# A two-layer diffusion step on one core: the first modulation vectors by matrix products, and a shorter last normalisation

## What is computed

```
m = silu(c) @ w_ada + b_ada                 # shift, scale, gate for each sublayer
u = x * (1 + scale) + shift
x = LN(ALPHA * x + res_w * gate * f(u))     # f: SwiGLU or mixing
```

## Time and profile before

| | |
|---|---|
| median of three runs | 2925.35 us (2923.78 to 2927.16) |
| the profiled execution: its own time | 2927.19 us |
| its span, first to last instruction | 2925.2 us |
| TensorE busy | 2786.0 us, 95% |
| VectorE busy | 1707.3 us, 58% |
| ScalarE busy | 774.8 us, 26% |
| mean granted TensorE clock | 0.983 of full speed |
| TensorE leaves the opening | at 117.93 us |
| the last reciprocal ends, the first block is multiplied | at 2904.08 us |

### The profile page before, as it was taken

How to read it: one execution, slowest core, us unless ns; L and a number is a source line. 1 busy time by engine, 2 the same in 40 slices (tenths; PEclk the granted TensorE clock), 3 DMA queues, 4 the chain that set the end, 5 groups by cost and what they waited for, 6 DMA issues and landing times.

```text
span 2925.2 us, 47407 instructions
## 1 busy us (share of the span) xinstructions
PE 2786.0 (95%) x18760; PEld 2740.6 (94%) x18760; DVE 1707.3 (58%) x3134; ACT 774.8 (26%) x1109; POOL 0.2 (0%) x4
## 2 busy tenths in 40 slices
PE   4899999899999999999999999989999999999994
PEld 4899999889999999999999999988989999999993
DVE  6654555753766773545586455575366568444456
ACT  3212111532322431111252111234232234111124
POOL 0000000000000000000000000000000000000000
PEclk8999999899999999999999999999999999999997
DMA  6343333112233232323223333321213322233220
GB/s 246 119 129 114 118 122 108 65 62 75 87 118 127 72 119 83 115 86 116 88 90 125 108 122 119 111 94 48 74 51 137 129 87 99 89 105 111 101 86 36
DMA packets 77061, 299.34 MB, mean 102 GB/s; under 512 B 24960, under 2 KB 29312, under 8 KB 52864
## 3 DMA queue, kind: packets, MB, share of 16 engines
q1 hardware_dynamic: 50688, 214.31, 21.0%
q10 hardware_dynamic: 26240, 83.20, 8.5%
HBM read 293.80 MB, written 6.82 MB: 103 GB/s over the span
## 4 chain that ended last, share of the span: by engine, by line
PE 89%; DVE 6%; issue 2%; ACT 1%; DMA 1%; SPq 0%; ACTq 0%; DVEq 0%
PE psum L588 12%; PE psum L590 12%; PE psum L591 12%; PE psum L406 6%; PE psum L409 6%; PE psum L408 6%; PE psum L451 3%; PE psum L454 3%; PE psum L455 3%; PE psum L808 3%; PE psum L810 3%; PE psum L811 3%; PE psum L492 2%; PE psum L497 2%; PE psum L496 2%
## 5 line engine op out<-in xcount | busy, mean ns | idle before, releaser
L588 PE MATMUL psum<-Uh,w_hi 128*128 128x320 f32 x2304 | 713.4, 310 | 8.9 <-DVE cst_l L1470 8.9
L590 PE MATMUL psum<-Ul,w_hi 128*128 128x320 f32 x2304 | 713.2, 310 | 0.0
L591 PE MATMUL psum<-Uh,w_lo 128*128 128x320 f32 x2304 | 713.0, 309 | 0.0
L872 ACT ACTIVATE w_hi<-w_raw 128x2048 fp32r<-128x2048 f32 x170 | 325.1, 1913 | 595.4 <-PE psum L406 318.8
L588 PEld LDWEIGHTS psum<-Uh,w_hi 128*128 128x128 f32 x2304 | 433.6, 188 | 9.2 <-issue 9.2
L1199 DVE TENSOR_TENSOR w_lo<-w_raw,w_hi 128x2048 fp32r<-128x2048 f32 x170 | 389.4, 2291 | 78.6 <-ACT w_hi L872 74.1
L590 PEld LDWEIGHTS psum<-Ul,w_hi 128*128 128x128 f32 x2304 | 433.7, 188 | 0.0
L591 PEld LDWEIGHTS psum<-Uh,w_lo 128*128 128x128 f32 x2304 | 433.6, 188 | 0.0
L1382 DVE TENSOR_TENSOR hf<-sg,psum 128x320 f32<-128x320 f32 x176 | 85.6, 486 | 407.6 <-ACT sg L960 406.1
L409 PE MATMUL psum<-Hh,w_lo 128*128 128x320 f32 x1024 | 316.2, 309 | 0.0
L406 PE MATMUL psum<-Hh,w_hi 128*128 128x320 f32 x1024 | 316.2, 309 | 0.0
(11 more groups left out here) (239 smaller groups left out, 5080.4 us busy)
## 6 DMA issues: line engine op xcount, KB each, us to landing
w_raw<-in_wstream SPq DMA_DIRECT2D x188, 1024.0 KB, 4.9
ada_w<-in_ada ACTq DMA_DIRECT2D x145, 512.0 KB, 3.6
first_w<-in_ada SPq DMA_DIRECT2D x15, 512.0 KB, 14.6
gath<-in_rpb SPq DMA_DIRECT2D x128, 24.0 KB, 3.3
G<-gath ACTq DMA_DIRECT2D x4, 768.0 KB, 4.5
X<-in_xT SPq DMA_DIRECT2D x8, 320.0 KB, 14.5
yT<-X SPq DMA_DIRECT2D x8, 320.0 KB, 3.4
mask<-in_mask ACTq DMA_DIRECT2D x2, 384.0 KB, 5.0
```

Source lines behind the costliest of these rows:

```text
L588: m1 = pe.matmul(out, wh, rh, start=(k == 0), stop=False)
L590: pe.matmul(out, wh, rl, start=False, stop=False)
L591: mm = pe.matmul(out, wl, rh, start=False, stop=(k == KD - 1))
L872: act.activation(hi, w_raw[:, r, :, :], ACT.Copy).then_inc(s_whi, 1)
```

## The change

Four things are changed.

1. The shift and scale of the first sublayer come from TensorE. c and c_ctx are loaded as columns (`ccol`, 128 x 8 x 2, 8 KB) and their silu `scol` is the moving operand of two columns; the slices of w_ada come in another layout (`ada_first`) and are the stationary operand. `mods_of(k)` makes 16 products in full f32 for block k into PSUM bank 6 or 7, and VectorE adds the bias in two small instructions (`first_mod`). All 16 slices now have buffers of their own, so no load waits. The two broadcasts are still needed by the sums of later sublayers; they are issued after block 4.
2. Both token halves of a block are made and used before the next block: three uses (tile 0 with both halves, tile 1 with the first) run block by block; tile 1 with the second half and the tiles 2 and 3 with both come after. The two weight tiles are loaded ahead of block 1.
3. TensorE's wait for the constants moves from the end of the opening to the first mixing.
4. In the last sublayer no u is made, by ScalarE or VectorE, in either half, and each half of each block is stored when it is ready, in 16 DMAs of 160 KB.

```diff
@@ SyncE
-            for k in range(2):
-                first_block(k)
+            first_block(0)
             for s in range(2):
                 sp.dma_start(w_raw[:, s, :, :], a["wstream"][s]).then_inc(s_wload[s], 16)
-            for k in range(2, 6):
+            for k in range(1, KD):
                 first_block(k)
-            sp.wait_ge(s_first, first_mods_ready(1, 1))
-            first_block(6)
-            first_block(7)
...
-            sp.wait_ge(s_y, DEPTH * PER_LAYER["y"])
-            for k in range(KD):
-                sp.dma_start(a["yT"][k], X[:, k, :]).then_inc(s_out, 16)
+            for h in range(2):
+                for k in range(KD):
+                    cols = slice(h * HT, (h + 1) * HT)
+                    sp.wait_ge(s_y, DEPTH * PER_LAYER["y"] - 2 * KD + (h * KD + k + 1))
+                    sp.dma_start(a["yT"][k][:, cols], X[:, k, cols]).then_inc(s_out, 16)
@@ TensorE, opening
+                def mods_of(k):
+                    pe.wait_ge(s_ada0[k], 32)
+                    if k == 0:
+                        pe.wait_ge(s_scol, 1)
+                    if k >= 2:
+                        pe.wait_ge(s_first, k - 1)
+                    for j in range(2):
+                        for c in range(KD):
+                            mm = pe.matmul(first_mods(k)[:, 2 * j:2 * j + 2], first_w[2 * k + j][:, c, :], scol[:, c, :],
+                                           start=(c == 0), stop=(c == KD - 1))
+                    mm.then_inc(s_fsum, 1)
...
+                mods_of(0)
+                mods_of(1)
                 tiles = [take(), take()]
...
                 for k in range(KD):
...
+                    if 1 <= k < KD - 1:
+                        mods_of(k + 1)
+                    pe.wait_ge(s_u, C["u"].at() + (2 * k + 1))
+                    block_products(tiles[0], us[0], 0, k)
+                    block_products(tiles[1], us[1], 0, k)
+                    pe.wait_ge(s_u, C["u"].at() + (2 * k + 2))
+                    block_products(tiles[0], us[2], 1, k)
+                one(tiles[1], 1)
+                late = take(spare_f)
+                one(late, 0, 2)
+                one(late, 1)
                 late = take(spare_h)
-                one(late, 0, 2)
-                one(late, 1, 1)
+                one(late, 0, 1)
+                one(late, 1)
                 C["u"].next(2 * KD)
-                pe.wait_ge(s_init, 4)
-                pe.wait_ge(s_cst, 64)
@@ ScalarE, finish
+                    if (l, s) != (DEPTH - 1, 2):
...
@@ VectorE, normalise
-                    split_u(h, k)
+                    if last:
+                        C["u"].next()
+                        C["u32"].next()
+                    else:
+                        split_u(h, k)
@@ VectorE, opening
+                def first_mod(k):
+                    dve.wait_ge(s_fsum, k + 1)
                     for j in range(2):
-                        if taken[0]:
-                            dve.wait_ge(s_first, taken[0])
-                        start_at = (bada[:, k:k + 1], lnm[:, 0, 0, k:k + 1])[j]
-                        dve.tensor_tensor_reduce(junk[:, :], first_w[(2 * k + j) % 12], csilu[:, v, :], 1.0, start_at,
-                                                 ALU.mult, ALU.add, mods[0][:, v, j * KD + k:j * KD + k + 1])\
-                            .then_inc(s_first, 1)
-                        taken[0] += 1
+                        i = dve.tensor_scalar(mods[0][:, :, j * KD + k], first_mods(k)[:, 2 * j:2 * j + 2],
+                                              (bada[:, k:k + 1], lnm[:, 0, 0, k:k + 1])[j], None, ALU.add)
+                    i.then_inc(s_first, 1)
```

More of the change, by code:

```diff
@@ L150, in build @@
         spare_o = [spare("spare_o0", 0, 8192), spare("spare_o1", 16384, 24576)]
-        craw = at("craw", 5120, [P, 2, D])
         cst = at("cst", 33792, [P, 4, P])
         warm = at("warm", 49152, [P, 1])
-        first_w = [at(f"first_w{i}", off, [P, D])[:, :] for i, off in enumerate(
-            (21504, 25600, 29696, 40960, 45056, 58880, 62976, 67072, 79360, 83456, 87552))]
-        first_w.append(ada_w[:, 1, :])
+        ccol = at("ccol", 49184, [P, KD, 2])
+        scol = at("scol", 49248, [P, KD, 2])
+        first_w = [at(f"first_w{i}", off, [P, KD, P])[:, :, :] for i, off in enumerate(
+            (21504, 25600, 29696, 40960, 45056, *range(51200, 92160, 4096)))]
+        first_w.append(ada_w[:, 1, :].rearrange("p (k n) -> p k n", k=KD))
         qT = at("qT", 0, [P, 2, T])
@@ L192, in bank, with first_mods @@
             return psum[p0:p1, 2 * (u % 4) + b, lo:hi]
[L194 to L198, removed]
+        def first_mods(k):
+            return psum[:, 6 + k % 2, 0:4]
         def scores(i, w):
@@ L231, in build @@
         s_csilu = sem("csilu_done")
+        s_ccol = sem("c_columns_loaded")
+        s_scol = sem("c_columns_silu")
+        s_fsum = sem("first_mods_summed")
         s_first = sem("first_mods")
@@ L546, in block_products @@
                         filled(mm)
+                mods_of(0)
+                mods_of(1)
                 tiles = [take(), take()]
-                us = [next_use(), next_use()]
+                us = [next_use() for _ in range(3)]
                 for k in range(KD):
[L551 to L563, removed]
+                    if 1 <= k < KD - 1:
[9 more added lines that the diff above has]
+                one(late, 1)
                 late = take(spare_h)
-                one(late, 0, 2)
-                one(late, 1, 1)
+                one(late, 0, 1)
+                one(late, 1)
                 C["u"].next(2 * KD)
-                pe.wait_ge(s_init, 4)
-                pe.wait_ge(s_cst, 64)
             def ffn(pending):
@@ L758, in fourier_pieces, with mixing @@
                 return piece
-            def mixing():
+            def mixing(first):
+                if first:
+                    pe.wait_ge(s_init, 4)
+                    pe.wait_ge(s_cst, 64)
                 tiles = [take(), take()]
@@ L841, in _ @@
                 ffn(l > 0)
[L842 removed]
+                mixing(l == 0)
                 ffn(True)
@@ L915, in finish @@
                     act.wait_ge(s_xn, C["xn"].next())
[L917 to L921, removed]
-                    C["u32"].next()
-                    act.wait_ge(s_u32, C["u32"].at())
+                    C["u32"].next()
+                    if (l, s) != (DEPTH - 1, 2):
+                        act.wait_ge(s_u, C["u"].at() + (h * KD + k - 3))
+                        for lo, hi, v in SEGS[h]:
+                            i = act.activation(u32[:, k % 4, lo - h * HT:hi - h * HT], X[:, k, lo:hi], ACT.Identity,
+                                               bias=lnm[:, v, 1, k:k + 1], scale=lnm[:, v, 0, k:k + 1])
+                        i.then_inc(s_u32, 1)
+                        act.wait_ge(s_u32, C["u32"].at())
                     col = l * (3 * KD) + (s * KD + k)
@@ L991, in first_input @@
                     for lo, hi, v in SEGS[h]:
-                        q = act.activation(u32[:, k % 4, lo - h * HT:hi - h * HT], X[:, k, lo:hi],
+                        q = act.activation(u32[:, i % 4, lo - h * HT:hi - h * HT], X[:, k, lo:hi],
                                            ACT.Identity, bias=mods[0][:, v, k:k + 1],
@@ L996, in first_input @@
                     act.wait_ge(s_u32, i + 1)
[L997 to L1003, removed]
+                    act.activation(Uh[:, k, h * HT:(h + 1) * HT], u32[:, i % 4, :], ACT.Copy).then_inc(s_fu, 1)
@@ L1004, in opening @@
+                act.dma_start(ccol[:, :, :], a["ccol"]).then_inc(s_ccol, 16)
+                act.dma_start(bada[:, :], a["bada"]).then_inc(s_bada, 16)
                 act.wait_ge(s_init, 1)
                 act.activation(warm[:, :], epsc[:, :], ACT.Silu)
+                act.wait_ge(s_ccol, 16)
+                act.activation(scol[:, :, :], ccol[:, :, :], ACT.Silu).then_inc(s_scol, 1)
+                for h in range(2):
+                    first_input(h, 0)
+                round_tile()
+                round_tile(1)
@@ new lines, in opening @@
+                for k in range(1, KD):
+                    for h in range(2):
+                        first_input(h, k)
+                    if k == 4:
+                        for v in range(2):
+                            act.dma_start(csilu[:, v, :], a["c" if v == 0 else "c_ctx"].partition_broadcast(P))\
+                                .then_inc(s_craw[v], 16)
+                round_tile(2, spare_f)
+                for _ in range(3):
+                    gate_half()
+                round_tile(2, spare_h)
@@ L1006, in opening @@
+                load_ada(FIRST_ADA, 0)
                 for v in range(2):
                     act.wait_ge(s_craw[v], 16)
[L1008 to L1011, removed]
+                    act.activation(csilu[:, v, :], csilu[:, v, :], ACT.Silu).then_inc(s_csilu, 1)
+                gate_half()
                 round_tile(1)
-                first_input(0, 2)
```

(25 more changed lines are left out.)

30 lines of the change are left out of this document (12 added, 18 removed).

## The result

The changed kernel takes 2903.38 us, the median of four runs (2901.2 to 2903.59), against 2925.4 us (2923.78 to 2927.16) before: a ratio of 0.9921 with an interval of 0.9908 to 0.9933, so 22 us less. The forecast was 2895.1, 30.2 us less; the time lies inside its range.

What follows compares the result with a forecast made beforehand. TensorE was busy 95% of the span, the opening bound by VectorE and by TensorE's waits at both its ends. Opening -12.5 and ending -17.7 make -30.2 us: 2895.1 us for the median, range 2886 to 2915.

Steps and rivals of the forecast that it cites:

- Rival 1: Opening: the clock falls in each burst and comes back, 2.7 us a step, 16 us for six, 2911 us; chance 0.31.
- (a): Ending, first half: leaving out eight pairs of rounding and subtracting on VectorE before the last mean gives -6.2 us.
- (b): Ending, second half: one ScalarE activation of 0.65 us a block, each block stored as it comes; -11.5 us, at most -12.5.
- (c): Opening, where TensorE starts: first burst and weight tiles replace the old waits, 25.5 us against 25.1; taken as 0 (-4 to +1).
- (d): Opening after the start: 384 products, 56.1 us, plus 1.5 at low clock and six bursts, 22.7; no waits for inputs.
- (e): Join of opening and loop: the wait for the constant goes, the loop's second weight tile comes just in time; 0, at most +1.
- Rival 2: Opening: the clock never returns, products and bursts stay at the low clock, +39.7 us, 2935 us; chance 0.06.
- Rival 3: Opening: cheaper bursts at 0.082 us a record, -7 us, and a start earlier by up to 4, 2884 us; chance 0.08.
- Rival 4: The opening gives nothing because inputs or weights come late in a new way; only the ending counts, 2907.6 us; chance 0.05.

## Why the prediction was right or wrong

**The whole.** The time lies in the range of 2886 to 2915, and the direction and the ending were forecast rightly. The opening was not: -12.5 us forecast, -2.0 measured. That the total still came out within 8.3 us is in part luck: the range had been drawn to take in Rival 1, which is what happened, and gains that stood in no term (2.6 us at the start, 2.7 at the loop, 2.3 in the ending) made up for over half of the 13 us that the clock cost.

**The ending, (a): right.** 6.2 us forecast, 6.2 measured, and TensorE's products were ready 5.3 us early, as said. **(b): undersized.** 11.5 forecast, 13.5 measured. I took ScalarE's 0.65 us an activation as its pace; back to back they start 0.54 us apart, so the last block is made 5.0 us after the first multiplication and not 5.7. The end of the span comes 2.65 us after that, where I had counted 0.67 for the last issue and 3.0 for landing: with the smaller transfer and SyncE already waiting, the tail is shorter. The upper bound of 12.5 was too low.

**(c), the start: inside its bounds, undersized.** I had taken no change; it is 22.46 in place of 25.1, -2.6 us, inside the bounds of -4 to +1. Block 0 was there at 6.0, not 8.85, and the first burst took 7 us and not 7.6.

**(d), the step that failed: "My sum holds if a burst of two-column products counts as work for the gate".** It doesn't. The path had 93.3 us where I had 80.3. With 64 columns the same path takes 79.7. So the count of products, the price of a record (0.109 at the full clock, against my 0.118) and the claim that neither inputs nor DMA would make TensorE wait were right, and the clock was the whole error, 13 us. Rival 1 is what happened, at a chance of 0.31 against the forecast's 0.50; the only thin work in the trace that spoke for the forecast were attention products with 64 columns, and between 64 columns and two is just where the experiment shows the difference. Rival 1's size, 2.7 us a step, was good: the steps cost 8.6 us instead of 6.2, 2.4 more. (By its own rows the part of a burst behind the 2.3 us of rest is 1.5 us and not 1.2, which would have made 3.0 a step and 2913.) Its 2911 was too high mainly because the start, the loop and the ending gained more than the sum had. The Trainium skill's rule that I weighed, in "TensorE: Matmul & The Clock Gate" under HAM oscillation, speaks of pauses between groups of matmuls; the trace agrees that the clock falls and returns at each step, with the difference that here TensorE shows no pause at all, and is busy to 100%.

**(e), the join: right, with one term missing.** The wait went, and the second tile came in time: no wait in the changed kernel, 0.16 us with the moved wait alone. What I left out was that the 8.9 us of idling had cost twice: the loop then ran its first 6 us at 1.2 GHz. The 2.7 us that come back there were in no term.

**Rivals.** Rival 2 (the clock never returns) fell: it returned in every step. Rival 3's price of 0.082 us fell too: a record with two columns costs 0.109 us at the full clock, no less than one with 64, so the trend from 128 to 64 columns does not go on. Rival 4 was nearly right in its number for the opening, by another cause than the one it names: no input and no tile is late.

The sum, then: -12.5 forecast for the opening against -2.0 measured by itself (in the traces -4.8: the -12.5 and +13.0 for the clock in the steps, -2.6 for the start, -2.7 for the restart), -17.7 against -20.0 for the ending.

**What stays open.** Executions of one kernel lie 1.3 to 4.6 us apart, and the 1.4 us behind the first mean in the two traces have no edit behind them. In all ten traces the stretch from the first mean to the one near 1006 us takes between 499.7 us (the changed kernel) and 501.2 us (the one before), and kernels with either opening stand at both ends, so it is scatter and not the change. It may be the moments at which the clock changes after each stop of TensorE, but no run was made on it. Nor was any width between 2 and 64 columns tried, nor what in a thin product lets the clock fall.

## What to carry to other kernels

Work that TensorE takes over from an engine that kept it waiting can have two prices, its own time and what it does to the granted clock of the dense products around it. TensorE busy for 100% of a stretch does not tell that the clock is up, so look at the clock of the stretch and at the step from one product to the next. In this kernel, padding such products with columns of zeros was faster than leaving them thin. And of a change with several parts, try the smallest alone: the moved wait of three lines was worth 10.9 us, and the rewritten opening around it had given all of that back.

The best kernel of this study is the one with 64 columns, 2889.99 us: 13.4 us under the changed one and 36 us under the one before.

## What I had not expected of the hardware

- A product of a full 128 x 128 f32 stationary operand with two moving columns fills TensorE's time and does not hold the clock: at 26.6 to 70.2 us the granted clock was 0.63 to 0.78 with TensorE 100% busy. With 64 columns the same products run at 1.00.
- The columns from 2 to 64 cost nothing. In the changed kernel the burst that begins at 53.08 runs at the full clock almost to its end (columns as for the bursts' stretches above, then the dense product that follows):

```profile
53.08:56.08 3.00, 3.00 (x30) 1.00 0.77 258
56.08:56.77 0.69, 0.69 (x6) 0.71 0.00 0
...
56.77 0.61 PE L552 MATMUL psum<-Uh,w_hi 128*128 128x320 f32 x1
```

A mean of 0.71 in the last 0.69 us means 0.40 us at half the clock, which is 0.20 us of work at the full one. So the burst of 3.69 us would take 3.49 us at the full clock, 0.109 us a record, as long as with 64 columns. The first burst, at 6.01, took 6.99 us, 0.22 a record, which is the low clock (the clock's column says 1.00 there, up to its first change, but the dense products from 22.46 on are 0.27 us apart as well).
- A 128x320 activation with scale and bias, 0.65 us in the record, starts 0.54 us after the one before where nothing else is on the engine.
